# Mixer layer of a two-layer decoder step: sample rows staged elsewhere, small steps of the last eight dense groups in another order

## What is computed

```python
def hybrid_mixer(h, pos, ret_s0, ssm_s0, conv_s0, w_in, w_out, ...):
    q, k, v, g, z, xbc_raw, dt_raw = jnp.split(h @ w_in, cuts, axis=-1)
    q = rope(q, pos); k = rope(k, pos) * (RET_DK ** -0.5)
    o_ret, ret_s = chunked_decay_recurrence(q, k, v, log_gamma, ret_s0)     # S = a S + k v^T, y = q S
    o_ret = o_ret * lax.rsqrt(jnp.mean(o_ret * o_ret, axis=-1, keepdims=True) + RMS_EPS)
    o_ret = o_ret.reshape(b, L, vv) * jax.nn.silu(g)
    xbc = jax.nn.silu(causal_depthwise_conv(xbc_full, conv_w, conv_b))
    xs, bm, cm = jnp.split(xbc, ...)
    dt = jax.nn.softplus(dt_raw + dt_bias)
    y, ssm_s = chunked_decay_recurrence(cm, bm, xs * dt, dt * a, ssm_s0)
    yg = ((y + d_skip * xs) * jax.nn.silu(z)).reshape(b, L, SSM_GROUPS, -1)
    yg = yg * lax.rsqrt(jnp.mean(yg * yg, axis=-1, keepdims=True) + RMS_EPS)
    mixed = jnp.concatenate([o_ret, yg.reshape(b, L, -1) * norm_w], axis=-1)
    return mixed @ w_out, ret_s, ssm_s, new_conv
```

## Time and profile before

| | us |
|---|---|
| median of 3 runs | 2424.82 |
| lowest and highest | 2419.87, 2424.89 |
| the profiled execution | 2422.35 |
| its span, first to last instruction | 2420.7 |
| TensorE busy in it | 2322.9 (96%) |
| VectorE, ScalarE, GpSimd busy | 1170.8, 762.2, 195.7 |
| hyb phase in it | about 440 to 904 |

### The profile page before, as it was taken

The page is one execution under the profiler, slowest core; times in us unless marked ns, Lnnn a source line. Parts: engine busy times, 40 slices in busy tenths (PEclk is TensorE's granted clock), DMA queues, the critical chain, the costliest instruction groups (busy, mean ns, idle before and its releaser), DMA issues.

```text
span 2420.7 us, 49208 instructions
## 1 busy us (share of the span) xinstructions
PE 2322.9 (96%) x19766; PEld 2258.1 (93%) x19766; DVE 1170.8 (48%) x1796; ACT 762.2 (31%) x1319; POOL 195.7 (8%) x232
## 2 busy tenths in 40 slices
PE   8999999889998899999999999999999989999997
PEld 8999999888787899999999999999988789999996
DVE  5444335765444535444345444335746635444434
ACT  4332323432223423332333233233223323322332
POOL 1000001132100000000000000001114400000000
PEclk9999999999998999999999999999999989999998
DMA  4233233222323222233332323334337712333332
GB/s 138 87 92 99 88 104 101 72 89 80 119 79 131 75 83 88 87 95 95 98 101 86 100 87 91 100 101 131 109 118 244 255 48 86 91 92 94 96 101 92
DMA packets 119473, 249.45 MB, mean 103 GB/s; under 512 B 15216, under 2 KB 15360, under 8 KB 118000
## 3 DMA queue, kind: packets, MB, share of 16 engines
q1 hardware_dynamic: 105408, 193.05, 26.7%
q0 software_dynamic: 13792, 54.43, 6.6%
q10 hardware_dynamic: 144, 0.09, 0.0%
HBM read 237.30 MB, written 9.95 MB: 102 GB/s over the span
## 4 chain that ended last, share of the span: by engine, by line
PE 69%; DVE 4%; issue 2%; ACT 1%; POOL 0%; POOLq 0%; DVEq 0%; ACTq 0%
PE psum L353 59%; PE psum L2095 1%; PE psum L2129 1%; DVE w_low L331 1%; PE psum L2121 1%; PE psum L1034 1%; PE psum L2065 1%; PE psum L2096 1%; PE psum L2039 1%; PE psum L2083 0%; PE psum L2004 0%; PE psum L370 0%; PE psum L1021 0%; DVE keys L2362 0%; PE psum L958 0%
## 5 line engine op out<-in xcount | busy, mean ns | idle before, releaser
L331 DVE TENSOR_TENSOR w_low<-w_raw,w_high 128x512 fp32r<-128x512 f32 x720 | 526.4, 751 | 655.1 <-ACT w_high L325 654.9
L353 PE MATMUL psum<-x_high,w_high 128*128 128x260 f32 x3872 | 786.6, 285 | 45.6 <-DVE w_low L331 18.9
L353 PE MATMUL psum<-x_low,w_high 128*128 128x260 f32 x3872 | 782.7, 284 | 0.0
L353 PE MATMUL psum<-x_high,w_low 128*128 128x260 f32 x3872 | 780.2, 283 | 0.0
L353 PEld LDWEIGHTS psum<-x_high,w_high 128*128 128x128 f32 x3872 | 599.0, 190 | 51.6 <-issue 17.0
L353 PEld LDWEIGHTS psum<-x_low,w_high 128*128 128x128 f32 x3872 | 603.0, 190 | 0.0
L353 PEld LDWEIGHTS psum<-x_high,w_low 128*128 128x128 f32 x3872 | 601.0, 190 | 0.0
L325 ACT ACTIVATE w_high<-w_raw 128x512 fp32r<-128x512 f32 x720 | 434.9, 623 | 515.1 <-PE psum L353 497.8
L353 PE MATMUL psum<-hidden_high,w_low 128*128 128x260 f32 x1408 | 284.0, 283 | 0.0
L353 PE MATMUL psum<-hidden_high,w_high 128*128 128x260 f32 x1408 | 283.2, 282 | 0.0
L353 PE MATMUL psum<-hidden_low,w_high 128*128 128x260 f32 x1408 | 282.9, 282 | 0.0
(11 more groups left out here) (344 smaller groups left out, 1760.8 us busy)
## 6 DMA issues: line engine op xcount, KB each, us to landing
w_raw<-in_weights_dram SPq DMA_DIRECT2D x720, 256.0 KB, 2.7
cache_pages<-in_cache_pages_dram POOLq DMA_DIRECT2D x128, 272.0 KB, 4.2
ret_sample_state<-in_state_ret_dram POOLq DMA_DIRECT2D x2, 2048.0 KB, 8.1
out_ret_s_dram<-ret_sample_state POOLq DMA_DIRECT2D x2, 2048.0 KB, 7.6
residual<-in_x_dram SPq DMA_DIRECT2D x4, 520.0 KB, 6.6
out_y_dram<-residual SPq DMA_DIRECT2D x8, 260.0 KB, 2.2
ssm_sample_state<-in_state_ssm_dram POOLq DMA_DIRECT2D x2, 1024.0 KB, 6.8
out_ssm_s_dram<-ssm_sample_state POOLq DMA_DIRECT2D x2, 1024.0 KB, 5.0
```

Of the source, the lines that this page charges most:

```text
L331: nc.vector.tensor_tensor(WL[:, slot, :], WRAW[:, slot, :], WH[:, slot, :].bitcast(F32), ALU.subtract).then_inc(w_split, 1)
L353: mm = nc.tensor.matmul(PS[:, b0 + 2 * m + half, 0:cols], w, x[:, half * cols:(half + 1) * cols], start=start, stop=stop)
```

## The change

**Sample rows.** The five sources of the small transfers get other addresses: `XDS` that of `YB`, the others in the zone of the convolution's tiles and of `SSS`. ScalarE's wait for all 24 transfers ahead of the first chunk is taken out. GpSimd loads the first four samples' `SSS` behind the 24 transfers, not ahead of the second wait for the convolution's stores; `chunk_end(0)` stands ahead of the wait for the transfers.

**Order.** ret y 0 moves from behind head 3 to behind head 2. ret outer 2 stands behind head 3, and then: hin 8, ret norm, ret outer 3, hin 9, ssm norm, ret y 1, ret spread, hin 10, ret yT (both halves in one step of 16 transposes), ssm spread, hin 11, hout 0 to 3. The samples' norm is no step of its own: its matmuls go into the banks of ssm spread ahead of tile 6 of hin 11, and tile 0 of hout 0 waits until VectorE has read them and inverted. Two steps fewer leave hout 0 and hout 1 on different bank sets. `YRB` becomes four tiles of 512 columns.

ScalarE, VectorE and GpSimd follow: the two roots are taken apart (retention first), the sample state update is divided, the second load of `S0` goes ahead of the store of the prompt's state, VectorE reads `gate_ret` products in other places, and the samples' gating, root, high and low parts are taken between the retention tiles.

```diff
@@ hyb_steps
+        if h == 2:
+            plan.step(("ret y", 0))
...
-    plan.step(("ret y", 0))
+    plan.step(("ret outer", 2))
     hin(8)
+    plan.step("ret norm")
+    plan.step(("ret outer", 3))
+    hin(9)
     plan.step("ssm norm")
-    plan.step("ret norm")
-    plan.step(("ret yT", 0))
-    hin(9)
-    plan.step(("ret outer", 2))
-    plan.step(("ret outer", 3))
+    plan.step(("ret y", 1))
     plan.step("ret spread")
     hin(10)
-    plan.step(("ret y", 1))
+    plan.step("ret yT")
     plan.step("ssm spread")
     hin(11)
-    plan.step(("ret yT", 1))
-    plan.step(("hout", 0), 8)
-    plan.step("ret sample norm")
-    for g in range(1, 4):
+    for g in range(4):
         plan.step(("hout", g), 8)
@@ tiles
-    YRB = at("ret_sample_out", [P, 1024], REGION + 29056)
+    YRB = [at("ret_sample_out0", [P, 512], REGION + 84640), at("ret_sample_out1", [P, 512], REGION + 103424)]
+    YRB2 = [at("ret_sample_out2", [P, 512], REGION + 29056), at("ret_sample_out3", [P, 512], REGION + 31104)]
...
-    XDS = at("ssm_x_samples", [NS, 1024], REGION + 66560)
-    XH8 = at("ssm_x_samples_high", [NS, 1024], REGION + 70656, F32R)
-    XL8 = at("ssm_x_samples_low", [NS, 1024], REGION + 82944, F32R)
-    BH8 = at("ssm_b_samples_high", [NS, P], REGION + 87040, F32R)
-    BL8 = at("ssm_b_samples_low", [NS, P], REGION + 87552, F32R)
+    XDS = at("ssm_x_samples", [NS, 1024], REGION + 101440)
+    XH8 = at("ssm_x_samples_high", [NS, 1024], ZONE + 12480, F32R)
+    XL8 = at("ssm_x_samples_low", [NS, 1024], ZONE + 16576, F32R)
+    BH8 = at("ssm_b_samples_high", [NS, P], ZONE + 27136, F32R)
+    BL8 = at("ssm_b_samples_low", [NS, P], ZONE + 27648, F32R)
@@ pe
+        def ret_sample_norm(k):
+            if k != 6:
+                return
+            wait_free(pe, "ssm spread")
             pe.wait_ge(sqm_done, 1)
...
+            mm.then_inc(rsn_full, 1)
...
+        ret_sample_outer(2)
+        hin(8)
+        ret_norm()
+        ret_sample_outer(3)
+        hin(9)
+        ssm_norm()
+        ret_sample_out(1)
+        ret_spread()
+        hin(10)
+        ret_sample_turns()
+        ssm_spread()
+        hin(11, before_k=ret_sample_norm)
...
         def ready(k):
+            if k == 0:
+                pe.wait_ge(rvs_done, 1)
             if k < 8:
                 pe.wait_ge(yl_done, k + 1)
-            if k == 4:
-                ret_sample_norm()
@@ act
-        act.wait_ge(xr_loaded, 16 * 24)
         for c in range(NTT):
...
+        a.splits(2)
+        silu_pair(("hin", 8), 4)
+        a.splits(2)
+        act.wait_ge(rv_done, 1)
+        nc.scalar.activation(RV[:], RV[:], ACT.Sqrt).then_inc(rr_done, 1)
+        a.splits(2)
+        silu_pair(("hin", 9), 5)
+        sample_rows_out(1)
+        a.splits(2)
+        act.wait_ge(sv_done, 1)
+        nc.scalar.activation(SV[:], SV[:], ACT.Sqrt).then_inc(sr_done, 1)
...
         act.wait_ge(rvs_done, 1)
         nc.scalar.activation(RVS[:], RVS[:], ACT.Sqrt).then_inc(rrs_done, 1)
+        a.splits(1)
+        silu_pair(("hin", 11), 7)
+        a.splits(1)
+        for t in range(6):
+            act.wait_ge(og_done, 1)
...
@@ dve
+            if i == 3:
+                sample_state(2)
...
         rstd_pair(("hin", 8), ZG[:, 0])
-        a.splits(2)
+        step = "ret norm"
+        wait_full(dve, step)
+        nc.vector.tensor_scalar(RV[:], PS[:, bank0(step), :], 1.0 / RDV, EPS, ALU.mult, ALU.add).then_inc(free(step), 1)
+        a.splits(2)
+        sample_state(3)
+        wait_free(dve, step)
+        nc.vector.reciprocal(RV[:], RV[:]).then_inc(rv_done, 1)
+        link(gate_ret(0))
+        a.splits(2)
...
         rstd_pair(("hin", 10), ZG[:, 0])
-        a.splits(2)
-        gate_ret(2).then_inc(og_done, 1)
+        sample_columns()
+        a.splits(2)
...
+        for t in range(8):
+            y_low(t)
+            if t in (1, 5):
+                a.splits(1)
+            if t == 4:
+                gate_ret(2).then_inc(og_done, 1)
+            if t == 6:
+                dve.wait_ge(rsn_full, 1)
+                link(nc.vector.tensor_scalar(RVS[:].rearrange("p h s -> p (h s)"), PS[:, bank0("ssm spread"), 0:RH * NS],
+                                             1.0 / RDV, EPS, ALU.mult, ALU.add))
+                nc.vector.reciprocal(RVS[:], RVS[:]).then_inc(rvs_done, 1)
+        a.splits(1)
+        rstd_pair(("hin", 11), ZG[:, 1])
@@ pool
-        pool.dma_start(SSS[:], io["state_ssm"][:, 0:4]).then_inc(sss_loaded, 16)
...
+        chunk_end(0)
         pool.wait_ge(xr_loaded, 16 * 24)
-        chunk_end(0)
+        pool.dma_start(SSS[:], io["state_ssm"][:, 0:4]).then_inc(sss_loaded, 16)
...
-        wait_free(pool, ("ret O", 3))
-        pool.dma_start(io["ret_p"], RST[:]).then_inc(rst_stored, 16)
         pool.wait_ge(s0_stored, 16)
         wait_full(pool, ("ret y", 0))
         pool.dma_start(S0[:], io["state_ret"][:, 4:8]).then_inc(s0_loaded, 16)
+        wait_free(pool, ("ret O", 3))
+        pool.dma_start(io["ret_p"], RST[:]).then_inc(rst_stored, 16)
```

More of the change, by code:

```diff
@@ L1157, in pe, with ssm_norm @@
-        mm.then_inc(full(step), 1)
-        hin(11)
-        ret_sample_turns(1)
-        def ret_sample_norm():
-            step = "ret sample norm"
-            acquire(pe, step)
+        def ssm_norm():
+            step = "ssm norm"
+            acquire(pe, step)
+            pe.wait_ge(ysq_done, 4)
+            for t in range(4):
+                for q in range(4):
+                    mm = nc.tensor.matmul(PS[32 * q:32 * q + 32, bank0(step), 0:TH], ONES[:, 0:32],
+                                          SQ[:, 4 * (q // 2) + t, (q % 2) * TH:(q % 2 + 1) * TH], start=t == 0, stop=t == 3)
+            mm.then_inc(full(step), 1)
@@ L1301, in sample_rows_out @@
             wait_full(act, step)
[L1302 removed]
+            if r:
                 act.wait_ge(rst_stored, 16)
             b = bank0(step)
[L1305 removed]
+            for half in range(2):
+                ins = nc.scalar.activation((YRB, YRB2)[r][half][:], PS[:, b + half, :], ACT.Copy)
+            ins.then_inc(free(step), 1)
         v_tokens(0)
```

169 lines of the change are left out of this document (72 added, 97 removed).

## The result

The changed kernel takes 2405.85 us, the median of four runs (2402.78 to 2410.82), against 2424.71 before: ratio 0.9931 [0.9914, 0.9947]. The forecast was 2403.0 within 2396 to 2412. The profiled execution took 2402.78 us around a span of 2401.1; the sum had given 2401.2 for such an execution. The medians are 18.9 us apart, where the sum was 21.2.

What follows compares the result with a forecast made beforehand. TensorE was taken as the bound, losing time to release waits and half clock. Sample rows -3.8 and tail -17.4 sum to -21.2 us: 2401.2 against the profiled execution, 2403.6 against the median; 2403.0 taken, range 2396 to 2412.

Steps and rivals of the forecast that it cites:

- What bounds the kernel: Whole kernel: TensorE is the bound; its stretch 727:834 holds 23 us that is not work, from holes and half clock.
- Part 2: Mixer tail, ret O 3 to hout 1: reordered steps cut holes from 15.0 to 3.9 us; 17.4 us with clock, bounds 10 and 20.
- the term of the clock: Mixer tail: of 8 us lost at half clock, 6.3 gained, with one half-clock piece of 3.4 us left.
- Table loads: ScalarE in the tail: three more loads of 1.28 us, 3.8 us together, costed at nothing beside 67 us free.
- Part 1: Ahead of hin 4, chunk 0: without ScalarE's wait for the sample rows, 3.8 us gained, ends 2.3 and 5.3.
- Cost nothing: GpSimd at chunks 0 and 1: later state load and the end-of-chunk product run at once add no time; load cover 2.8 us.
- Rival (e): Behind the stretch: gains are taken back, so no change; argued that nothing there can take 20 us; chance 0.02.
- The first sign: Ahead of hin 4: the hole should be 5 to 5.5 us, ended by VectorE's product.
- (a): Tail: VectorE falls behind one group earlier, release waits return at two boundaries, 7.2 us less gained, 2410; chance 0.15.
- (b): Tail: the clock keeps its slow pieces though holes are short, 6.3 + 1.5 us less, 2411; chance 0.08.
- (c): Tail: ScalarE's table loads land on the path, 4 to 5 us, 2408 (2411 by the skill page's figure); chance 0.06.
- (d): Tail: VectorE's in-order queue becomes the bound, 34.5 us of loss against 23, 7.7 slower, 2432; chance 0.02.

Runs made afterwards that it cites:

- e2: Changed kernel with the sample-row addresses, ScalarE's wait and GpSimd's order put back as before, leaving only the new order: 2407.82 us, 0.9936.
- e10: Changed kernel with the second half of VectorE's sample state update moved behind its gates' read of hin 9: 2410.51 us, 0.9955.
- again: The changed kernel run once more, unaltered, for a second trace: 2407.41 us (six runs), 0.9937.
- e4: Changed kernel with GpSimd's end-of-chunk product put behind the wait for the rows alone: 2403.97 us, 0.9924.
- e12: Changed kernel with only GpSimd's log tile and mask of chunk 1 held until VectorE has released chunk 0's scores: 2405.99 us, 0.9917.
- e3: Changed kernel with GpSimd's end-of-chunk product behind the wait for the rows, the state load and VectorE's release of the scores: 2407.22 us, 0.9943.
- e8: Changed kernel with GpSimd's end-of-chunk product behind VectorE's release of the scores, ahead of the wait for the rows: 2402.97 us, 0.9910.
- e1: Kernel before with only the new sample-row addresses, no ScalarE wait and GpSimd's new order: 2419.77 us (ten runs), 0.9994.
- e5: Changed kernel with the samples' mean taken behind the third low part, VectorE's gate product behind all eight: 2401.9 us, 0.9917.
- e9: Changed kernel with e8 and e5 together, state load between GpSimd's two pieces, samples' high and low parts sooner: 2402.76 us, 0.9926.
- e11: Kernel before with the sample-row change and GpSimd's order of e8, nothing of the new tail order: 2422.86 us (twelve runs), 0.9992.

## Why the prediction was right in sum and wrong in a part

**What bounds the kernel: right.** TensorE is the bound in both, and the 23 us of 727:834 that were not work are what was won: 20.5 us net in the profiled execution.

**Part 2: right, in its holes nearly to the tenth.** Foreseen were 0.7 ahead of hin 8, 0.2 (hin 9), 0.1 (hin 10) and 2.4 (hout 0); the trace has 0.72, 0.14, 0.13 and 2.33. The 3.2 us in hout 0 and the 1.3 behind it are gone. From the end of ret O 3 to hout 1 it took 84.0 us, foreseen 87. The sum was too small by 3.1 (17.4 against 20.5), mostly in the term of the clock: the holes gave 11.7 (15.0 less 3.3), so the clock and the rest 8.8, where I had 6.3. I left one piece of half clock and 0.97; the stretch had none and 1.00, and the retention spread, which had taken 2.09 us at half clock, took 1.14. e2 shows that this part alone gives the measured gain; e10 shows the hole that comes back when VectorE's work stands elsewhere. In the six other traces of this order it is 16.2 (again), 17.5 (e2, e4), 19.1 (e12), 20.4 (e3) and 20.5 (e8). So 17.4 lies inside, near the lower end, and where one piece of half clock stayed by hout 0, as in again, e2, e4 and e12, the clock of the stretch is 0.98, close to the 0.97 foreseen.

**Table loads: right.** Six loads of 1.28 us, 7.7 us on ScalarE, and neither wait left in the stretch is for a ScalarE activation behind one: the 0.72 is a read of ret O 3. The rule of the Trainium skill ("ScalarE: Activation LUTs", "Table sets: the hidden batching unit") doesn't set the time here, where ScalarE is idle over half of the stretch (busy 41.75 of 85 us).

**Part 1: the failed step is "Cost nothing".** I gave ScalarE's wait its 4.1 us and said that GpSimd's product "now runs at once", as if it were alone. It runs beside VectorE's splits and its product. The earlier trace rows held the warning: VectorE's product from 539.63 to 541.61 lies over GpSimd's from 538.63 to 540.52, and ends 1.09 us after it; its 1.98 us were 1.2 of work and 0.8 of waiting. The same trace has the price alone, two chunks later; beside GpSimd's copy, in chunk 1, it is 1.73:

```profile
563.87 1.73 DVE L1530 TENSOR_TENSOR ssm_c_decayed<-ssm_bc,ssm_c_decayed 128x1024 f32<-128x1024 f32 x1 [0.58 <-ACT ssm_c_decayed L1261]
```

```profile
587.44 1.23 DVE L1530 TENSOR_TENSOR ssm_c_decayed<-ssm_bc,ssm_c_decayed 128x1024 f32<-128x1024 f32 x1 [0.57 <-ACT ssm_c_decayed L1261]
```

I took 1.98 as its length and gave it a place where GpSimd has three instructions in a row. The holes of 8.15 and 12.73, and of 4.48 once GpSimd is held, show it from both sides.

The Trainium skill has this rule: its page "SBUF — State Buffer", section "Who interferes with whom", says that a VectorE instruction with two inputs in SBUF contends with a GpSimd instruction that reads SBUF, and that the one that issues first has the shared port for the whole instruction, while the other is blocked. The traces agree: L1552, with one input in PSUM, stays at 0.41; L1554, with two in SBUF, is 1.22 alone and 2.58, 3.17 or 7.76 beside GpSimd. The page would let the product in when the one GpSimd instruction is through; that it sat out three is more than the rule says.

**Why the sum held: partly luck.** In the first trace, part 1's stretch gave 4.0 us where 3.8 was written, though only 2.2 of it at the place I meant (stage 28.0 to 25.8), and of those 1.2 are the hole. In the other traces with this GpSimd order (again, e1, e5, e10) the stage is 3.0 to 3.7 us longer than before. Outside the stage the same stretch varies by itself: e2, which has the rows of before and 27.7, is still 3.4 us longer up to ret O 3, ret y 0 deducted, with 17.8 us at half clock between hin 4 and there where before has 11.9 and after 6.3. What hid this in the total is part 2's surplus and the rest of the program. There 5.0 us were given back in the first trace, a term I had at nothing.

**The rest of the program.** Rival (e) said that nothing behind the stretch could take gains back, since its code and its bound stay. Some of them it does take, in some executions. Stretches of 60 us in the mla phase, before and after:

```profile
1740.00:1800.00 60.00, 57.86 (x401) 55.19 (x401) 30.43 (x53) 10.12 (x14) 8.58 (x16) 0.91 0.44 146
```

```profile
1715.50:1775.50 60.00, 57.86 (x387) 55.76 (x386) 30.25 (x53) 9.35 (x14) 8.61 (x16) 0.86 0.45 146
```

The same busy time, with 14 matmuls fewer at a granted clock of 0.86. The group of 64 small matmuls in it (busy us, mean ns), of before, after and e5_norm_first:

```profile
L2004 PE MATMUL psum<-queries,w_uk_by_head 64*128 64x8 f32 x64 | 10.6, 305 | 1.4 <-issue 1.4
```

```profile
L2036 PE MATMUL psum<-queries,w_uk_by_head 64*128 64x8 f32 x64 | 13.2, 348 | 1.4 <-issue 1.4
```

```profile
L2035 PE MATMUL psum<-queries,w_uk_by_head 64*128 64x8 f32 x64 | 10.4, 302 | 1.4 <-issue 1.4
```

The new order is not needed for it. e1_rows_only, with the tail of before, has the long form too:

```profile
L2003 PE MATMUL psum<-queries,w_uk_by_head 64*128 64x8 f32 x64 | 13.3, 350 | 1.4 <-issue 1.4
```

It goes by where the low clock falls: the rest holds 34.1 us at half clock in before (651.6 us), 36.3 in e5 (650.3), 45.7 in after (656.6) and 51.2 in e3 and e8 (659). Why it falls there is not shown. Over the 13 traces the rest takes 650.2 to 659.1, while the code is the same. This is as large as what part 1 could give.

**The signs that I had named.** "Wrong if TensorE waits for the state load": it doesn't. "A hole over 1.5 ahead of hin 9, 10 or 11": none. "Clock near 0.9": 1.00 in the first trace, 0.98 in the second. The first sign, a hole of 5 to 5.5 us ahead of hin 4, is the one that failed. Rivals (a), (b), (c) and (d) didn't come. e10 shows what (a) would have been: one release late, a hole of 3.9 us. The lower end of the range was added up a little low: 2424.8 less 25.3 and 2.5 is 2397.0, not 2396.

**What stays open.** What each move of part 2 gives: it was run as a whole, and only the places of the state update (e10) and of the samples' mean (e5) were varied by themselves. Why VectorE's product is let in between GpSimd's instructions in one execution and not in the next. Why the two splits take 2.99 us although most of it lies ahead of the recorded start of GpSimd's product (the second split, at 534.4, should take 0.69 and ends at 536.8, 0.4 us after that start); in the traces where that product is not directly behind the issues of the rows, the pair takes 1.28. And why the runs of the unaltered change fall between 2399.8 and 2412.4: only one of those six was traced, the 2412.4 with the 12.73 hole, so that the long hole belongs to the slower runs is a guess. What is on record is the granted clock of each whole execution: 0.980 to 0.982 in the three above 2411, 0.984 to 0.985 in the three below 2404.

## What to carry to other kernels

Before GpSimd's arithmetic is moved, list VectorE's instructions with both inputs in SBUF that will lie beside it: each can last until GpSimd is through, and the cheap remedy is to let GpSimd wait for VectorE's release rather than start as soon as it can. It halved the hole here; a gain in the total of this kernel was too small to show. A duration taken from a trace is a price only if nothing lay beside it: look at the same instruction in other chunks. When the bound engine waits for releases between its large steps, walk the reading engine's queue step by step with its traced durations; it gave the four holes here to 0.1 us, and half or more of the time at half clock left with them. A gain under 5 us in one trace of this kernel says little by itself, since identical later phases differ by up to 9 us between traces: compare the stage, and leave the total to many runs.

## What the runs showed of the hardware

- A VectorE product of 128x1024 with both inputs in SBUF takes 1.21 to 1.23 us alone and 1.73 to 7.76 beside GpSimd's products and copies. It ends 1.09 us after the last of GpSimd's that held it (before, again, e1, e5, e10, e12; 1.68 in the first trace of the change, where a transfer's issue follows). A split of 128x512 ends 0.56 us after it (e3, e4, e8, e9, e11). GpSimd's copy of 128x1024 is held in its turn: 2.01 instead of 1.05 us.
- A VectorE product of 128x256 with one input in PSUM takes 0.41 us in the same place.
- With 11.7 us of holes in the tail removed, the granted clock there rose from 0.90 to 1.00 (0.98 in four other traces), but the pieces at half clock in the whole program went only from 94.2 to 81.7 us: some of them now stand elsewhere (20.3 us near the end instead of 15.7).
